# Output projections tile by tile, with logits held token by partition, in a two-layer attention and expert step on one core

## The chip, the cores and the metric

The kernel runs on one core of a Trainium2 chip. The metric is the device time of one execution in microseconds. Before the change the median of three runs is 1421.58 us (1417.67 to 1422.39).

## The reference

The step computes two layers for 512 prompt tokens and 64 sample tokens (8 sequences of 8), each of width 1024, in float32. Layer 0 mixes with forgetting attention (prompt, and samples against a paged cache), layer 1 with an mLSTM. After each mixer comes the part that the change touches:

```python
xp = xp + mixed_p @ w_out            # and the same for xs; 1024 x 1024
h  = rmsnorm(x, norm_ffn[layer])     # x * rsqrt(mean(x*x) + eps) * g
g_logits = h @ w_group + b_group     # 4 groups
e_logits = h @ w_router + b_router   # 4 x 8 experts
# best group, its two best experts, softmax weights of the two
# y = sum over the two experts of silu(h @ w_gate) * (h @ w_up) @ w_down
```

After the second layer a last rmsnorm gives the outputs. Keys, values, forget logs and states are outputs too; the change doesn't touch them.

## The kernel before

The program is a row of phases. In each, the five engines have an instruction list of their own, tied by semaphores, and all meet at its end. `out_and_experts` (L1020) is the phase after each mixer, so it runs twice. Tokens lie in five tiles: four of 128 prompt tokens (0 to 3) and one of 64 samples (tile 4, called L in the code). `turned` holds the mixer's result with features on partitions, in KC = 8 chunks; `x` and `rows` hold tokens on partitions. PSUM has eight banks of 512 floats; `ps2` views them as four pairs of 1024.

**Products.** `multiply_out` (L1225) runs over the eight chunks outside and the four prompt tiles inside, so all four tiles fill four bank pairs together and all are complete only in the last chunk. The samples follow in the pair of tile 0 once that was read: their two column halves lie in the two partition halves of the array. In layer 1 the weight chunks arrive from memory just ahead (L1128) and lie in the third expert slot; in layer 0 they were loaded in the phase before (`w0_in`).

**Norm.** For each tile: VectorE adds the product to `x` (`add_tile` L1469, `add_samples` L1474); ScalarE squares and sums (`square` L1396, which writes `rows` as scrap); VectorE makes the mean (`mean` L1456); GpSimd raises it to -0.5 (L1200); ScalarE scales `x` into `rows` (`scale` L1402); SyncE's queue stores `rows` to memory (`keep_row_tile` L1121), from where the experts' tokens are gathered later. TensorE flips the tile in eight transposes (`flip` L1244), and VectorE multiplies by the gain, back into `turned` (`keep_gained` L1461).

**Logits.** `logits` (L1258) multiplies with the router weights as the stationary operand (64 columns, of which 36 are used and 28 are cleared) and the tokens as the moving one. Even chunks go to the upper partition half and odd ones to the lower, so the result is logits by token, in two half sums. When all five tiles are in, VectorE adds the bias and copies them to SBUF (L1509), and TensorE adds the halves and turns them to tokens on partitions, with five products by a folding matrix (L1272). TensorE's order is written out by hand in `pe_` (L1330): products, flip 0, flip 1, then logits and flips alternately.

**Routes.** `routes` (L1482) on VectorE picks groups and experts, in small dependent steps from L1491 on, with TensorE counting ranks (L1276, L1278), building the lists (L1284) and the overflow lists (L1291). `idle_products` (L184) are products nobody reads, put between. Then GpSimd gathers the tokens of the first two pairs of experts (L1185), which waits for the lists (`index_ready`) and for all stored rows (`kept`).

**Experts.** Sixteen pairs of experts, of 6 MB of weights each, go through three slots. Pairs 0 and 1 are loaded at the phase's start. Pair 2's gate and up weights (L1140) wait for all products, since layer 1's output weights lie there, and its down weights (L1145) for all flips and for `kept`, since they overwrite `rows`. The gate and up weights of pair 3 wait for half of pair 0's products (`gu_half`, L1310), and so on, slot by slot.

Of the kernel before, what the change touches and what calls it, by code (L numbers as in the profile page):

```python
# [16 lines left out]
ALU = mybir.AluOpType  # L17
# [3 lines left out]
P = 128  # L21
# [95 lines left out]
def trunk(nc, i, o):  # L117

    with ExitStack() as ctx:
# [900 lines left out]
        def out_and_experts(layer, w_dram, w_early=None):  # L1020
# [5 lines left out]
            SLOTS = 3  # L1026
            gu = [sb(tag + f"gu{s}", [P, 2, 2, KC, HID], where=mx) for s in range(SLOTS)]
# [9 lines left out]
            lb = sb(tag + "lb", [P, 1], where=mx)  # L1037
# [14 lines left out]
                  for k, n in enumerate(("en", "ea", "both8"))}  # L1052
# [16 lines left out]
            cleared_, wr_in, lg_done, lT_kept, lg_turned = (sem(tag + "cleared"), sem(tag + "wr_in"), sem(tag + "lg_done"),  # L1069
                                                            sem(tag + "lT_kept"), sem(tag + "lg_turned"))  # L1070
# [50 lines left out]
            def keep_row_tile(sp, n):  # L1121

                sp.wait_ge(scaled, n + 1)
                sp.dma_start(h_dram[layer][n * P:n * P + ROWS[n], :], rows[0:ROWS[n], n, :]).then_inc(kept, 16)

            def sp_(sp):
                for c in range(KC if layer else 0):
                    sp.dma_start(w[:, c, :], w_dram[c * P:(c + 1) * P, :]).then_inc(w_in[c], 16)  # L1128
                sp.wait_ge(cleared_, 2)
                sp.dma_start(wr[:, :, 0:GROUPS], i["moe_w_group"][layer].rearrange("(p c) n -> p c n", c=KC)).then_inc(wr_in, 16)  # L1130
                sp.dma_start(wr[:, :, GROUPS:LG], i["moe_w_router"][layer].rearrange("(p c) n -> p c n", c=KC)).then_inc(wr_in, 16)
                sp.dma_start(lb[0:GROUPS, :], i["moe_b_group"][layer:layer + 1, :].rearrange("a n -> n a"), allow_slow_non_contiguous=True).then_inc(wr_in, 16)
                sp.dma_start(lb[GROUPS:LG, :], i["moe_b_router"][layer:layer + 1, :].rearrange("a n -> n a"), allow_slow_non_contiguous=True).then_inc(wr_in, 16)
# [91 lines left out]
            def multiply_out(pe):  # L1225

                if layer:
                    idle_products(pe, 4, 0)
                for c in range(KC):
                    pe.wait_ge(w_in[c], 16)  # L1230
                    for n in range(L):
                        for half in range(2):
                            mm = pe.matmul(ps[:, 2 * n + half, :], turned[:, c, n * P:(n + 1) * P],  # L1233
                                           w[:, c, half * 512:half * 512 + 512], start=(c == 0), stop=(c == KC - 1))
                        if c == KC - 1:
                            mm.then_inc(multiplied, 1)
                pe.wait_ge(added, 1)
                for c in range(KC):
                    for half in range(2):
                        mm = pe.matmul(ps[half * SAMP:(half + 1) * SAMP, half, :], turned[:, c, PROMPT:TOK],  # L1240
                                       w[:, c, half * 512:half * 512 + 512], start=(c == 0), stop=(c == KC - 1))
                mm.then_inc(multiplied, 1)

            def flip(pe, n):  # L1244

                r = ROWS[n]
                pe.wait_ge(scaled, n + 1)
                if n < 2:
                    pe.wait_ge(added, n + 2)
                elif n < L:  # L1250
                    pe.wait_ge(gained, n - 1)
                else:
                    pe.wait_ge(added, L + 2)
                for c in range(KC):
                    mm = pe.transpose(ps2[:, (1, 2, 1, 2, 0)[n], c * P:c * P + r], rows[0:r, n, c:D:KC], ident[0:r, 0:r])
                mm.then_inc(flipped, 1)

            def logits(pe, n):  # L1258

                r = ROWS[n]  # L1260
                pe.wait_ge(gained, n + 1)
                for c in range(KC):
                    half = c % 2
# [1350 lines left out]
```

## Time and profile before

| | |
|---|---|
| median of 3 runs | 1421.58 us |
| lowest, highest | 1417.67, 1422.39 us |
| profiled execution, its own time | 1428.57 us |
| span of its trace | 1426.7 us |
| TensorE products busy | 1237.4 us (87%) |
| TensorE weight loads busy | 654.8 us (46%) |
| VectorE, ScalarE, GpSimd busy | 26%, 17%, 15% |
| memory traffic | 322.18 MB read, 31.31 MB written |

A busy TensorE is one with a product in flight, idle products among them; its share says nothing of which stage sets the end. That is read from the chain of waits and from the timeline of the stage.

### The profile page before, as it was taken

How to read it: one execution, taken by the hardware profiler on the slowest of the kernel's cores; microseconds unless marked ns; L12 is line 12 of the kernel's file. 1: busy time of each engine (PE TensorE's matmuls, PEld its weight loads, DVE VectorE, ACT ScalarE, POOL GpSimd, SP SyncE). 2: the span in 40 equal slices, each digit the busy share in tenths (PEclk: the TensorE clock that was granted, in tenths of full speed). 3: DMA queues.
4: the chain of work that ended last, by engine and by line, in shares of the span. 5: the costliest groups of instructions: out<-in, count | busy, mean ns of one | idle time of the engine just before them, and what ended most of it. 6: DMA issues, size and time to landing. Idle time of an engine off the chain costs nothing.

```text
span 1426.7 us, 16246 instructions
## 1 busy us (share of the span) xinstructions
PE 1237.4 (87%) x6285; PEld 654.8 (46%) x6285; DVE 370.4 (26%) x793; ACT 246.7 (17%) x572; POOL 214.4 (15%) x268
## 2 busy tenths in 40 slices
PE   8999999879699899778868999998879989977790
PEld 5764575557444533233324764444744543333330
DVE  4231003545311621111114400112710541111115
ACT  2000004653200201000003201014410300100001
POOL 2300002322100111111001000212920011111102
PEclk9999999999999999988988999999989999998995
DMA  8320504859975689999957130303148579999965
GB/s 282 102 62 7 179 13 137 266 183 362 344 282 224 250 302 420 419 419 420 410 221 270 60 105 18 121 12 82 39 146 352 190 253 417 419 420 419 419 277 207
DMA packets 103676, 339.96 MB, mean 238 GB/s; under 512 B 21454, under 2 KB 40082, under 8 KB 79786
## 3 DMA queue, kind: packets, MB, share of 16 engines
q1 hardware_dynamic: 88456, 302.84, 55.8%
q0 software_dynamic: 14848, 35.94, 7.0%
q8 instruction: 53, 0.87, 0.3%
q14 instruction: 29, 0.24, 0.1%
q10 hardware_dynamic: 290, 0.07, 0.0%
HBM read 322.18 MB, written 31.31 MB: 248 GB/s over the span
## 4 chain that ended last, share of the span: by engine, by line
PE 54%; SPq 16%; DMA 12%; DVE 7%; issue 4%; POOL 3%; ACT 2%; POOLq 2%; DVEq 0%; ACTq 0%
SPq L1096 10%; PE ps L1819 8%; PE ps L1233 8%; PE ps L1308 7%; PE ps L458 4%; DMA moe_gu<-in_moe_w_up 4%; SPq L1118 4%; PE ps L436 4%; PE ps L1770 4%; DMA fox_arena<-negs_rows 3%; PE ps L1326 3%; PE ps L351 2%; DMA moe_wd<-in_moe_w_down 1%; PE ps L748 1%; PE ps L1830 1%
## 5 line engine op out<-in xcount | busy, mean ns | idle before, releaser
L1308 PE MATMUL ps<-moe_gu,rows 128*64 128x512 f32 x1024 | 243.6, 630 | 57.1 <-DMA moe_gu<-in_moe_w_up 53.8
L1308 PEld LDWEIGHTS ps<-moe_gu,rows 128*64 128x64 f32 x1024 | 80.5, 145 | 199.8 <-issue 191.1
L1819 PE MATMUL ps<-mwblk,turned 128*128 128x512 f32 x256 | 111.5, 593 | 2.2 <-DVE vaug L2022 1.5
L1595 DVE TENSOR_TENSOR turned<-turned,ps 128x256 f32<-128x256 f32 x32 | 13.5, 421 | 304.7 <-ACT turned L1411 304.7
L1192 POOL DMA_INDIRECT expert_rows<-turned,moe_row x32 | 32.1, 1004 | 392.3 <-ACT turned L1421 358.8
L1326 PE MATMUL ps<-moe_wd,moe_rowsel 128*64 128x512 f32 x352 | 80.4, 598 | 2.3 <-DMA moe_wd<-in_moe_w_down 1.3
L1819 PEld LDWEIGHTS ps<-mwblk,turned 128*128 128x128 f32 x256 | 48.0, 190 | 61.1 <-issue 57.4
L1411 ACT ACTIVATE turned<-ps 128x256 f32<-128x256 f32 x32 | 12.3, 384 | 302.4 <-PE ps L1308 302.4
L458 PE MATMUL ps<-turned,fox_arena 128*128 128x288 f32 x256 | 62.3, 406 | 0.0
L436 PE MATMUL ps<-fox_arena,turned 128*128 128x512 f32 x128 | 59.0, 619 | 2.9 <-issue 2.9
L1233 PE MATMUL ps<-fox_arena,turned 128*128 128x512 f32 x128 | 55.2, 593 | 0.7 <-DVEq L2564 0.7
L351 PE MATMUL ps<-turned,fox_arena 128*128 128x288 f32 x224 | 55.2, 406 | 0.0
L1233 PE MATMUL ps<-moe_gu,turned 128*128 128x512 f32 x128 | 55.2, 593 | 0.0
L458 PEld LDWEIGHTS ps<-turned,fox_arena 128*128 128x128 f32 x256 | 48.6, 190 | 14.1 <-issue 0.8
L1770 PE MATMUL ps<-turned,mwblk 128*128 128x288 f32 x224 | 54.5, 406 | 0.0
L237 POOL TENSOR_TENSOR fox_arena<-fox_arena,cst 128x256 f32<-128x256 f32 x32 | 23.0, 728 | 201.2 <-DMA fox_arena<-negc_rows 201.0
L186 PE MATMUL ps<-cst 128*128 128x512 f32 x68 | 40.0, 731 | 9.5 <-POOLq L2564 8.3
L1770 PEld LDWEIGHTS ps<-turned,mwblk 128*128 128x128 f32 x224 | 42.6, 190 | 11.8
L351 PEld LDWEIGHTS ps<-turned,fox_arena 128*128 128x128 f32 x224 | 42.2, 190 | 11.4
L1600 DVE COPY turned<-ps 128x512 f32<-128x512 f32 x32 | 22.1, 691 | 88.0 <-PE ps L1326 88.0
L1185 POOL DMA_INDIRECT turned<-h_rows,moe_row x32 | 33.2, 1038 | 76.6 <-DVE moe_row L1554 44.1
L928 DVE CUSTOM_DVE_ANT_0 fox_arena<-ps,fox_arena 128x128 f32<-128x128 f32 (+3 forms) x64 | 28.2, 479 | 62.9 <-PE ps L725 62.9
(357 smaller groups left out, 1567.5 us busy)
## 6 DMA issues: line engine op xcount, KB each, us to landing
moe_gu<-in_moe_w_gate SPq DMA_DIRECT2D x56, 1024.0 KB, 22.3
moe_gu<-in_moe_w_up SPq DMA_DIRECT2D x56, 1024.0 KB, 23.9
moe_wd<-in_moe_w_down SPq DMA_DIRECT2D x44, 1024.0 KB, 25.0
rows<-in_moe_w_down SPq DMA_DIRECT2D x20, 1024.0 KB, 22.9
fox_arena<-in_cache_v POOLq DMA_DIRECT2D x32, 512.0 KB, 13.1
fox_arena<-in_fox_w_in SPq DMA_DIRECT2D x6, 2048.0 KB, 10.3
mwblk<-in_mlstm_w_in SPq DMA_DIRECT2D x6, 2048.0 KB, 8.6
fox_arena<-in_cache_k SPq DMA_DIRECT2D x20, 512.0 KB, 9.7
```

What stands on the lines that cost most here:

```text
L186: pe.matmul(ps[:, bank, :], ident, const("ones")[:, 0:512], start=True, stop=True)
L351: mm = pe.matmul(ps[:, 2 * (g % 3) + half, 0:HT], wblk[:, g // 4, c, (g % 4) * P:(g % 4 + 1) * P], turned[:, c, half * HT:(half + 1) * HT] ...
L436: mm = pe.matmul(ps[:, m % 4, :], turned[:, c, n * P:(n + 1) * P], wblk[:, (2 + blk) % 3, c, :], start=(c == 0), stop=(c == KC - 1))
L458: mm = pe.matmul(ps[:, 2 * ((g + 2) % 4) + half, 0:HT], wblk[:, (4 + g // 4) % 3, c, (g % 4) * P:(g % 4 + 1) * P], turned[:, c, half * HT: ...
L1096: sp.dma_start(gu[p % SLOTS][:, half, k], i[name][layer, 2 * p + half].rearrange("(p c) n -> p c n", c=KC)).then_inc(gu_in[p % SLOTS], 16)
L1118: sp.dma_start(wd[p % SLOTS][:, half], i["moe_w_down"][layer, 2 * p + half].rearrange("(p c) n -> p c n", c=2)).then_inc(down_in[p % SLOTS ...
L1185: pool.indirect_dma_start(xg[:, s, :], None, h_dram[layer], bass.IndirectOffsetOnAxis(ap=rows_of(0, p), axis=0), bounds_check=TOK - 1, oob ...
L1233: mm = pe.matmul(ps[:, 2 * n + half, :], turned[:, c, n * P:(n + 1) * P], w[:, c, half * 512:half * 512 + 512], start=(c == 0), stop=(c == ...
L1308: mm = pe.matmul(ps[h, 2 + p % 2, :].rearrange("s (k f) -> s k f", k=2), xT[:, c, h], gu[s][:, half, :, c, :], start=(c == 0), stop=(c == ...
L1326: mm = pe.matmul(ps[h, 5 + n, :], aT[p % 2][:, m, h], wd[s][:, half, m, n * 512:(n + 1) * 512], start=(m == 0), stop=(m == 1))
L1770: mm = pe.matmul(ps[:, bank + half, 0:HT], wblk[:, k % 3, c, g * P:(g + 1) * P], turned[:, c, half * HT:(half + 1) * HT], start=(c == 0), ...
L1819: mm = pe.matmul(ps[:, m % 4, :], turned[:, c, n * P:(n + 1) * P], wblk[:, k % 3, c, :], start=(c == 0), stop=(c == KC - 1))
```

## The change

The five tiles are taken in the order 0, 1, 2, L, 3. The products of a tile run over all eight chunks before the next tile's begin, and TensorE's flips and logits of earlier tiles stand between them; the products of tile 3 are cut in two halves, with flip L and logits 2 between. Three bank pairs serve products and flips in turn. Logits have the tokens as the stationary operand (128 columns) and the router weights as the moving one (36 columns), and the bias comes in by a product of one row of ones with the bias row, so the result stands with tokens on partitions in bank 6; the copy to SBUF and the fold are gone. Clearing `wr` and `lb`, and SyncE's wait for it, are gone. Four idle products stand ahead of flip 3. In the diff `AT[n]` is a tile's place in the order, counted from 1. `ps2` pairs and `rows` are as before.

```diff
+            ORDER = (0, 1, 2, L, 3)
+            AT = {n: k + 1 for k, n in enumerate(ORDER)}
+            MUL_PAIR, TURN_PAIR = {0: 0, 1: 2, 2: 1, L: 0, 3: 2}, {0: 0, 1: 2, 2: 1, L: 0, 3: 1}
-            lb = sb(tag + "lb", [P, 1], where=mx)
+            lb = sb(tag + "lb", [1, LG], where=mx)
...
             def sp_(sp):
-                sp.wait_ge(cleared_, 2)
...
-                for n in range(L - 1):
+                for n in ORDER[0:NT - 1]:
                     keep_row_tile(sp, n)
                 sp.wait_ge(multiplied, NT)
                 load_gate_up(sp, 2)
-                keep_row_tile(sp, L - 1)
-                keep_row_tile(sp, L)
+                keep_row_tile(sp, ORDER[NT - 1])
...
             def pool_(pool):
-                pool.memset(wr[:], 0.0).then_inc(cleared_, 1)
-                pool.memset(lb[:], 0.0).then_inc(cleared_, 1)
-                for n in range(NT):
-                    pool.wait_ge(meaned, n + 1)
+                for n in ORDER:
+                    pool.wait_ge(meaned, AT[n])
...
+            def multiply_out(pe, n, chunks):
+                b = 2 * MUL_PAIR[n]
+                if n == L:
+                    pe.wait_ge(gained, AT[0])
+                elif n == 3:
+                    pe.wait_ge(gained, AT[1])
+                for c in chunks:
+                    pe.wait_ge(w_in[c], 16)
+                    for half in range(2):
+                        cols = slice(half * 512, half * 512 + 512)
+                        to = ps[:, b + half, :] if n < L else ps[half * SAMP:(half + 1) * SAMP, b + half, :]
+                        mm = pe.matmul(to, turned[:, c, n * P:n * P + ROWS[n]], w[:, c, cols], start=(c == 0), stop=(c == KC - 1))
+                if c == KC - 1:
+                    mm.then_inc(multiplied, 1)
+
+            def flip(pe, n):
+                r = ROWS[n]
+                pe.wait_ge(scaled, AT[n])
+                if n == 3:
+                    pe.wait_ge(gained, AT[2])
                 for c in range(KC):
+                    mm = pe.transpose(ps2[:, TURN_PAIR[n], c * P:c * P + r], rows[0:r, n, c:D:KC], ident[0:r, 0:r])
+                mm.then_inc(flipped, 1)
+
+            def logits(pe, n):
+                r = ROWS[n]
+                pe.wait_ge(gained, AT[n])
+                if r < P:
+                    pe.matmul(ps[r:P, 6, n * LG:(n + 1) * LG], const("ones", 1)[:, 0:P - r], lb[:], start=True, stop=True)
+                pe.matmul(ps[0:r, 6, n * LG:(n + 1) * LG], const("ones", 1)[:, 0:r], lb[:], start=True, stop=False)
                 for c in range(KC):
-                    half = c % 2
-                    mm = pe.matmul(psf[half * SLOT:(half + 1) * SLOT, 6 * 512 + n * P:6 * 512 + n * P + r], wr[:, c, :],
-                                   turned[:, c, n * P:n * P + r], start=(c < 2), stop=(c >= KC - 2))
+                    mm = pe.matmul(ps[0:r, 6, n * LG:(n + 1) * LG], turned[:, c, n * P:n * P + r], wr[:, c, 0:LG],
+                                   start=False, stop=(c == KC - 1))
                 mm.then_inc(lg_done, 1)
 
             def route(pe):
-                pe.wait_ge(lT_kept, 2)
-                for n in range(NT):
-                    mm = pe.matmul(ps[:, 0, n * LG:(n + 1) * LG], lT[:, n * P:(n + 1) * P], const("fold"), start=True, stop=True)
-                mm.then_inc(lg_turned, 1)
                 idle_products(pe, 5, 4)
...
             def pe_(pe):
-                multiply_out(pe)
+                if layer:
+                    idle_products(pe, 4, 7)
+                multiply_out(pe, 0, range(KC))
+                multiply_out(pe, 1, range(KC))
                 flip(pe, 0)
+                multiply_out(pe, 2, range(KC))
                 flip(pe, 1)
                 pe.wait_ge(wr_in, 64)
-                pe.wait_ge(added, L)
                 logits(pe, 0)
+                multiply_out(pe, L, range(KC))
                 flip(pe, 2)
                 logits(pe, 1)
+                multiply_out(pe, 3, range(KC // 2))
+                flip(pe, L)
+                logits(pe, 2)
+                multiply_out(pe, 3, range(KC // 2, KC))
+                logits(pe, L)
+                idle_products(pe, 4, 7)
                 flip(pe, 3)
-                logits(pe, 2)
-                flip(pe, 4)
                 logits(pe, 3)
-                logits(pe, 4)
                 route(pe)
...
             def act_(act):
+                for n in ORDER:
                     square(act, n)
+                    scale(act, n)
...
             def routes(dve):
                 dve.wait_ge(lg_done, NT)
-                dve.tensor_scalar(lT[:, 0:TOK], psf[:, 6 * 512:6 * 512 + TOK], lb[:, 0:1], None, ALU.add).then_inc(lT_kept, 1)
-                dve.wait_ge(lg_turned, 1)
-                lg = ps[:, 0, 0:NT * LG].rearrange("p (n e) -> p n e", e=LG)
+                lg = ps[:, 6, 0:NT * LG].rearrange("p (n e) -> p n e", e=LG)
...
             def dve_(dve):
+                add_tile(dve, 0)
+                mean(dve, 0)
+                add_tile(dve, 1)
+                keep_gained(dve, 0)
+                mean(dve, 1)
+                add_tile(dve, 2)
+                keep_gained(dve, 1)
+                mean(dve, 2)
+                add_tile(dve, L)
+                keep_gained(dve, 2)
+                mean(dve, L)
+                keep_gained(dve, L)
+                add_tile(dve, 3)
+                mean(dve, 3)
+                keep_gained(dve, 3)
                 routes(dve)
```

## Rows read from the trace of the kernel before

**Rows 1.** The page, the chain that ended last, shares of the span by line.
```profile
SPq L1096 10%; PE ps L1819 8%; PE ps L1233 8%; PE ps L1308 7%; PE ps L458 4%; DMA moe_gu<-in_moe_w_up 4%; SPq L1118 4%; PE ps L436 4%; PE ps L1770 4%; DMA fox_arena<-negs_rows 3%; PE ps L1326 3%; PE ps L351 2%; DMA moe_wd<-in_moe_w_down 1%; PE ps L748 1%; PE ps L1830 1%
```
**Rows 2.** The chain in order of time (start us, us, what), layer 0's phase.
```profile
408.42 55.17 PE ps L1233 x128
463.59 7.04 PE ps L1240 x32
...
569.60 2.89 SPq L1096
```
**Rows 3.** Timeline: start us, us, engine, line, tiles, records [idle before <-releaser]; both layers.
```profile
408.42 7.96 PE L1233 MATMUL ps<-fox_arena,turned 128*128 128x512 f32 x18 [0.70 <-DVEq L2564]
...
483.55 0.18 DVE L1491 TENSOR_REDUCE moe_gmax<-ps 128x5 f32<-128x20 f32 x1 [1.40 <-PE ps L1272]
...
1059.98 2.41 PE L1233 MATMUL ps<-moe_gu,turned 128*128 128x512 f32 x5
...
1135.15 0.18 DVE L1491 TENSOR_REDUCE moe_gmax<-ps 128x5 f32<-128x20 f32 x1 [1.40 <-PE ps L1272]
```
**Rows 4.** Timeline of layer 0, flips, logits and fold after the products.
```profile
470.54 2.05 PE L1255 MATMUL ps<-cst,rows 128*128 128x128 f32 x16
...
474.48 1.16 PE L1255 MATMUL ps<-cst,rows 128*128 128x128 f32 x8
475.57 1.09 PE L1264 MATMUL ps<-turned,moe_wr 128*64 128x128 f32 x16
...
481.34 0.82 DVE L1509 TENSOR_SCALAR moe_lT<-ps,moe_lb 128x576 f32<-128x576 f32 x1 [0.81 <-PE ps L1264]
...
482.21 1.30 PE L1272 MATMUL ps<-cst,moe_lT 128*128 128x36 f32 x10 [0.92 <-DVE moe_lT L1509]
...
483.35 4.54 PE L186 MATMUL ps<-cst 128*128 128x512 f32 x10
```
**Rows 5.** Timeline of layer 0, the norm's chain: one full tile's add, then the samples' steps.
```profile
460.19 1.22 DVE L1472 TENSOR_TENSOR x<-x,ps 128x1024 f32<-128x1024 f32 x1 [0.42 <-PE ps L1233]
...
472.09 1.06 ACT L1400 ACTIVATE rows<-x 64x1024 f32<-64x1024 f32 x1 [3.25 <-DVE x L1479]
...
473.50 0.55 POOL L1200 TENSOR_TENSOR rstd<-ms,cst 128x1 f32<-128x1 f32 x1 [5.94 <-DVE ms L1459]
...
474.08 1.15 ACT L1406 ACTIVATE rows<-x,rstd 64x1024 f32<-64x1024 f32 x1 [0.85 <-POOL rstd L1200]
...
475.68 1.23 DVE L1465 TENSOR_TENSOR turned<-ps,gains 128x1024 f32<-128x1024 f32 x1 [1.12 <-PE ps L1255]
```
**Rows 6.** Timeline of layer 0, SyncE's queue and GpSimd's gather.
```profile
470.64 0.33 SPq L1096 DMA_DIRECT2D moe_gu<-in_moe_w_gate  x1
...
472.79 2.97 SPq L1124 DMA_DIRECT2D h_rows<-rows  x2
...
487.88 0.81 SPq L1118 DMA_DIRECT2D rows<-in_moe_w_down  x2
...
496.10 1.14 POOL L1185 DMA_INDIRECT turned<-h_rows,moe_row  x1 [22.05 <-DVE moe_row L1554]
```
**Rows 7.** Output weights: timeline of their issues, then layer 1's median us to landing.
```profile
397.70 4.11 SPq L659 DMA_DIRECT2D fox_arena<-in_fox_w_out  x6
...
1054.71 5.55 SPq L1128 DMA_DIRECT2D moe_gu<-in_mlstm_w_out  x8
...
moe_gu<-in_mlstm_w_out SPq DMA_DIRECT2D x8, 512.0 KB, 7.9
```
**Rows 8.** Timeline, idle products and transposes where the granted clock is half.
```profile
494.79 3.56 PE L186 MATMUL ps<-cst 128*128 128x512 f32 x4
...
1051.55 1.97 PE L2273 MATMUL ps<-cst,mstaged 128*128 128x128 f32 x8 [6.28 <-DVE mstaged L2459]
```
**Rows 9.** One-us windows, layer 0: busy of PE, PEld, DVE, ACT, POOL; clock, DMA, GB/s.
```profile
478.00:479.00 1.00, 1.00 (x19) 0.83 (x13) 1.00 (x1) 0.00 (x0) 0.00 (x0) 1.00 1.09 451
...
491.00:492.00 1.00, 0.00 (x0) 0.00 (x0) 0.93 (x3) 0.00 (x0) 0.00 (x0) 0.59 0.98 410
```

More of the change, by code:

```diff
@@ L1121, in keep_row_tile @@
             def keep_row_tile(sp, n):
-                sp.wait_ge(scaled, n + 1)
+                sp.wait_ge(scaled, AT[n])
                 sp.dma_start(h_dram[layer][n * P:n * P + ROWS[n], :], rows[0:ROWS[n], n, :]).then_inc(kept, 16)
@@ L1423, in act_ @@
             def act_(act):
-                for n in range(L):
+                for n in ORDER:
                     square(act, n)
-                    if n:
-                        scale(act, n - 1)
-                scale(act, L - 1)
-                square(act, L)
-                scale(act, L)
+                    scale(act, n)
                 act.wait_ge(to_exp, 1)
@@ L1463, in keep_gained @@
                 r = ROWS[n]
-                dve.wait_ge(flipped, n + 1)
+                dve.wait_ge(flipped, AT[n])
                 dve.tensor_tensor(turned[:, :, n * P:n * P + r],
-                                  ps2[:, (1, 2, 1, 2, 0)[n], :].rearrange("p (c t) -> p c t", t=P)[:, :, 0:r],
+                                  ps2[:, TURN_PAIR[n], :].rearrange("p (c t) -> p c t", t=P)[:, :, 0:r],
                                   gain.unsqueeze(2).broadcast_to([P, KC, r]), ALU.mult).then_inc(gained, 1)
             def add_tile(dve, n):
-                dve.wait_ge(multiplied, n + 1)
-                dve.tensor_tensor(x[:, n, :], x[:, n, :], ps2[:, n, :], ALU.add).then_inc(added, 1)
-            def add_samples(dve):
-                dve.wait_ge(multiplied, NT)
-                for half in range(2):
-                    cols = slice(half * 512, half * 512 + 512)
-                    dve.tensor_tensor(x[0:SAMP, L, cols], x[0:SAMP, L, cols], ps[half * SAMP:(half + 1) * SAMP, half, :], ALU.add
-                                      ).then_inc(added, 1)
+                dve.wait_ge(multiplied, AT[n])
+                b = MUL_PAIR[n]
+                if n < L:
+                    ins = dve.tensor_tensor(x[:, n, :], x[:, n, :], ps2[:, b, :], ALU.add)
+                else:
+                    for half in range(2):
+                        cols = slice(half * 512, half * 512 + 512)
+                        ins = dve.tensor_tensor(x[0:SAMP, L, cols], x[0:SAMP, L, cols], ps[half * SAMP:(half + 1) * SAMP, 2 * b + half, :], ALU.add)
+                ins.then_inc(added, 1)
             def routes(dve):
@@ L1606, in dve_ @@
                     dve.wait_ge(x_again, 16 * (NT - 1))
-                for n in range(L):
-                    add_tile(dve, n)
-                    if n:
-                        mean(dve, n - 1)
-                mean(dve, L - 1)
-                add_samples(dve)
-                keep_gained(dve, 0)
+                add_tile(dve, 0)
+                mean(dve, 0)
+                add_tile(dve, 1)
+                keep_gained(dve, 0)
+                mean(dve, 1)
[4 more added lines that the diff above has]
+                keep_gained(dve, 2)
                 mean(dve, L)
-                for n in range(1, NT):
-                    keep_gained(dve, n)
+                keep_gained(dve, L)
+                add_tile(dve, 3)
+                mean(dve, 3)
+                keep_gained(dve, 3)
                 routes(dve)
```

38 lines of the change are left out of this document (6 added, 32 removed).

## The prediction

> **What bounds the kernel now.** I read the page first. In its chain that ended last, the largest line is the loading of expert weights, and the output products (L1233) hold 8% of the span [rows 1]. The chain in order of time then shows how the phase is tied together: products of the four prompt tiles, products of the samples, a chain of small steps, and from about 570 us on SyncE's issues of weights [rows 2]. From there memory sets the pace, but a slot is only free, and the stream only starts, once pair 0 of the experts has been multiplied. So whatever moves the start of pair 0 moves the whole stream behind it, one to one, and nothing later gives it back. The question is therefore one distance, read in the timeline: from the first output product to the first step of the routes on VectorE. It is 483.55 - 408.42 = 75.13 us in layer 0 and 1135.15 - 1059.98 = 75.17 us in layer 1 [rows 3]. The two layers do the same, so I work one out and double it.
>
> What fills the 75.13 us is TensorE. Its products end at 470.54, which is 62.12 us after the start. From there to 483.55 are 13.01 us, and they hold the flips and logits of all five tiles, back to back but for short waits, then the copy and the fold [rows 4]. The norm of tiles 0 to 3 is already hidden: adds, squares and scales run on the other engines while TensorE multiplies tile 3 and the samples. What the change puts "under" the products are flips and logits, and these are TensorE's own work. They can't run beside products on the same engine; they only change places with them. That is the core of my forecast.
>
> **The change, part by part.**
>
> Products: the same 62.12 us, in another order. Four prompt tiles take 55.17 us, 13.79 each, and the samples the rest [rows 2].
>
> Flips: eight transposes took from 474.48 to 475.57, so 1.09 us [rows 4]. Flips 0, 1, 2 and L now stand ahead of the last product: 4 x 1.09 = 4.36 us.
>
> Logits: their form is new. Before, a tile took 1.09 us (16 records of 64 stationary columns, 475.57 on) [rows 4]. Now it takes eight products with 128 stationary and 36 moving columns, and one more for the bias. The nearest row is the fold: 128 stationary and 36 moving columns, five products in 10 records, from 482.21 to the next engine row at 483.35 [rows 4]. That is 1.14 / 10 = 0.114 us a record, and 9 products make 18 records: 2.05 us a tile. The ends are 1.09 us (no dearer than before) and 18 x 1.09 / 8 = 2.45 us (as dear as a transpose record). I take 2.05, since shape and type are the same. Logits 0, 1 and 2 ahead of the last product: 6.15 us. The last product then ends 62.12 + 4.36 + 6.15 = 72.63 us after the start.
>
> Waits in that stretch: flip 0 needs the norm of tile 0, some 4.6 us after its products by the chain below, and has tile 1's 13.79 us for it. The same holds for flips 1, 2 and L, with 6.9 us at the least. Products into a reused bank pair wait for gains that VectorE ended several us earlier. All at nothing. Behind a wait that failed here, all of TensorE would queue, so this cover matters.
>
> The tail: tile 3 is now alone at the end, and its whole norm lies open. Handover to VectorE about 0.15; add 1.22; handover 0.1; from the start of the square to that of the power 473.50 - 472.09 = 1.41; to the scale 0.58; scale 1.15 [rows 5]. That is 4.61 us to scaled rows. Beside it run logits L (estimated 1.2, with half the columns) and four idle products (4 x 0.91 = 3.6 by ten records in 4.54) [rows 4]: 4.8 us, so they end with the chain and cost 0.2 at the most; I count nothing. Then handover 0.1, flip 3 until VectorE starts 475.68 - 474.48 = 1.20, the gain 1.23 [rows 4, 5], handover 0.14, and logits 3 with their drain 2.25. Tail: 9.53 us. The routes begin 72.63 + 9.53 = 82.16 us after the start, against 75.13: **7.03 us later in each layer.**
>
> Removed: the copy (L1509) and the fold, 483.55 - 481.34 = 2.2 us [rows 3, 4], which the sum has by leaving them out. The routes themselves keep their length; the five idle products start in the same relation to them. Clearing `wr` and `lb` was beside products and brings nothing.
>
> Queues: SyncE has stored the other four tiles by then, and issues pair 2's loads at the last product, then tile 3's rows. Before, loads issued at 470.64 and rows behind them until 475.76 let `kept` through at 487.88, 17.2 us later [rows 6]. Now the same bytes but the samples' follow, so `kept` comes some 17 us after 72.63, at 89.8 after the start. The gather's start was 496.10 - 408.42 = 87.7 [rows 6], and is 94.7 after. So 4.9 us of slack are left, where there were 8. Pair 2's down weights, held by the same wait, are sent 7 us before the gather now and 8 before; they may brush it. I put 0.2 us on each layer, between 0 and 1.5.
>
> First products: tile 0 now takes a weight chunk each 13.79 / 8 = 1.72 us, not each 6.9. In layer 0 the last chunks were issued by 401.81, and the last is needed at 420.5. In layer 1 the last is issued by 1060.3; chunks take 7.9 us to land, so 1068.2, and it is needed at 1072.0 [rows 3, 7]. Nothing at the one end; 1.5 us, once, at the other, if chunks 1 to 3 land together. I take nothing.
>
> **Sum.** 2 x (7.03 + 0.2) = 14.5 us. The profiled execution's own time is 1428.6 us (span 1426.7), which gives 1443.1. It lies 7.0 us above the median of 1421.58; the same steps on the median give **1436.0 us**, 1.0% slower.
>
> **A rule weighed.** While flips and logits ran without a break, the granted clock stayed at its upper level, as in the window at 478 us; it fell at 491 us, behind a stretch in which TensorE had little to do [rows 9]. The Trainium skill, TensorE: Matmul & The Clock Gate, in its part on PE-mode transpose, says that transposes don't count as busy in the way products do, so the clock would not rise for them. The first of these windows disagrees, as far as flips mixed with logits go.
>
> **The rivals.**
>
> *Cheap logits.* If 36 moving columns are what counts and a tile takes 1.09 us, four tiles save 4 x 0.96 = 3.8 us a layer, 7.7 in all: 1428.3 us. For it: fewer moving columns than before. Against it: the fold's records, of the same shape.
>
> *All hidden, so faster.* Weight loads are drawn beside products, and if the inserted flips and logits ran under the 512-column products at no cost, the routes would begin after 62.12 + 9.53 = 71.65 us, 3.5 earlier than now: 1421.6 - 7.0 = 1414.6 us. It decides if the inserted work costs under 3.5 us of its 10.5. Against it: flips and logits stood end to end with each other, 1.09 us each, never overlapped [rows 4]. This is the case on the other side.
>
> *The clock falls in the tail.* Tile 3's tail is sparse, as the stretch before 491 us was. At the lower level eight transposes took 1.97 us instead of 1.16 [rows 4, 8], the logits could take 2.05 more, and an idle record 0.89 instead of 0.45 [rows 4, 8], so five idle products could outlast the routes' first steps by some 3.7. All three together are 6.5 us a layer; I price half, 3.3: 1442.6 us. Against it: the four idle products stand just ahead. By the skill's rule above this case is likelier, since flip 3 would not hold the clock; that sentence moves no number.
>
> *`kept` takes over.* If the rows of tile 3, queued behind 4 MB of loads, take over 22 us instead of 17.2, GpSimd's gather waits for them, and everything behind it. At 24.5 us it is 2.4 a layer: 1440.8 us. Against it: the order and sizes in the queue are as before.
>
> *The change does less than it says.* If TensorE's reorder left the end of products where it is, and the tail alone grew or shrank to match the 13.0 us, the time would stay at 1421.6. Nothing in the rows gives that.
>
> **How the numbers follow.** Forecast 0.74 (own range 1432 to 1440, from the logits' upper end, 4 x 0.4 x 2 = 3.2, and the small terms), cheap logits 0.09, clock 0.08, `kept` 0.04, all hidden 0.03, no effect 0.02. The range runs from just under the cheap logits, 1428, to just over `kept`, 1442. About 0.3% is what a measurement of this kernel can tell from no change, 4.3 us. Faster 0.03, same 0.03, slower 0.94.
>
> **What would show it.** Right: the first step of the routes 82 us after the first output product in both layers; a full tile's logits near 2.05 us; TensorE without a wait from start to the last product at 72.6; square, power and scale of tile 3 with nothing of worth beside them; the weights' stream unchanged but 7 and 14 us later. Wrong: a distance of 78 (logits cheap) or under 75 (hidden), a clock at half level between the last product and the routes, or GpSimd's gather released by stored rows.

## The result and the profile after the change

The changed kernel takes 1443.33 us (median of 4 runs, 1431.42 to 1445.92) against 1421.46 us before. The ratio is 1.0137, with a 95% interval from 1.0092 to 1.0182: **slower by 1.4%**, some 19.5 us by the ratio. The profiled execution took 1445.92 us, its span is 1443.8 us.

The first thing to read is the same distance as before, from the first output product to the first step of the routes, and then on to pair 0 of the experts. The timeline of layer 0 on TensorE (start us, us, engine, line, tiles, records, idle before):

```profile
404.56 27.70 PE L1235 MATMUL ps<-fox_arena,turned 128*128 128x512 f32 x64 [0.71 <-DVEq L2557]
432.10 1.05 PE L1246 MATMUL ps<-cst,rows 128*128 128x128 f32 x8
...
446.72 1.05 PE L1246 MATMUL ps<-cst,rows 128*128 128x128 f32 x8
447.70 0.41 PE L1255 MATMUL ps<-moe_lb,cst 1*128 1x36 f32 x2
448.04 1.98 PE L1257 MATMUL ps<-moe_wr,turned 128*128 128x36 f32 x16
449.94 7.09 PE L1235 MATMUL ps<-fox_arena,turned 128*64 128x512 f32 x32
...
460.19 7.11 PE L1235 MATMUL ps<-fox_arena,turned 128*128 128x512 f32 x16
467.24 1.09 PE L1246 MATMUL ps<-cst,rows 64*128 64x64 f32 x8
...
470.40 8.81 PE L1235 MATMUL ps<-fox_arena,turned 128*128 128x512 f32 x16
479.14 0.24 PE L1254 MATMUL ps<-moe_lb,cst 1*64 1x36 f32 x1
...
480.43 3.70 PE L186 MATMUL ps<-cst 128*128 128x512 f32 x8
483.97 1.04 PE L1246 MATMUL ps<-cst,rows 128*128 128x128 f32 x8
486.33 0.41 PE L1255 MATMUL ps<-moe_lb,cst 1*128 1x36 f32 x2 [1.32 <-DVE turned L1457]
486.67 2.46 PE L1257 MATMUL ps<-moe_wr,turned 128*128 128x36 f32 x16
488.94 7.45 PE L186 MATMUL ps<-cst 128*128 128x512 f32 x10
...
509.60 5.80 PE L1297 MATMUL ps<-moe_gu,rows 128*64 128x512 f32 x26 [0.74 <-DVE rows L1578]
```

From the first product to the end of logits L at 480.43 us no row has idle time before it, so TensorE is the bound of that stretch, as forecast. Behind it stand the four idle products, beside the norm of tile 3. Flips and logits stand between the products, each with its own time. The two halves of tile 3's products are the same work, but the first runs from 460.19 to 467.24 (7.05 us) and the second from 470.40 to 479.14 (8.74 us). The last product ends 74.58 us after the start, not 72.63.

VectorE, SyncE's queue and GpSimd around the tail, the same timeline:

```profile
479.25 1.22 DVE L1466 TENSOR_TENSOR x<-x,ps 128x1024 f32<-128x1024 f32 x1 [10.19 <-PE ps L1235]
479.25 0.34 SPq L1098 DMA_DIRECT2D moe_gu<-in_moe_w_gate  x1
...
482.50 1.15 ACT L1402 ACTIVATE rows<-x,rstd 128x1024 f32<-128x1024 f32 x1 [0.84 <-POOL rstd L1198]
...
489.17 0.18 DVE L1482 TENSOR_REDUCE moe_gmax<-ps 128x5 f32<-128x20 f32 x1 [2.89 <-PE ps L1257]
...
495.20 0.80 SPq L1120 DMA_DIRECT2D rows<-in_moe_w_down  x2
...
502.56 1.13 POOL L1185 DMA_INDIRECT turned<-h_rows,moe_row  x1 [20.10 <-DVE moe_row L1543]
```

The routes begin 489.17 - 404.56 = 84.61 us after the start, against 75.13 [rows 3]. Layer 1 shows the same, on TensorE and VectorE:

```profile
1066.65 27.63 PE L1235 MATMUL ps<-moe_gu,turned 128*128 128x512 f32 x64
...
1132.42 8.81 PE L1235 MATMUL ps<-moe_gu,turned 128*128 128x512 f32 x16
...
1151.04 0.18 DVE L1482 TENSOR_REDUCE moe_gmax<-ps 128x5 f32<-128x20 f32 x1 [2.74 <-PE ps L1257]
...
1172.54 7.82 PE L1297 MATMUL ps<-moe_gu,rows 128*64 128x512 f32 x32
```

There it is 84.39 us. Where pair 0 of the experts began before, in the chain that ended last (start us, us, what):

```profile
503.13 7.09 PE ps L1308 x32
...
1154.73 7.09 PE ps L1308 x32
```

From the start to pair 0 it was 94.71 and 94.75 us before; now it is 105.04 and 105.89. That is 10.33 + 11.14 = 21.5 us more, and the median rose by 21.9. What follows pair 0 kept its length: from layer 0's pair 0 to layer 1's first product it was 556.85 us and is 557.05, and from layer 1's pair 0 to the end of the span 272.0 and 271.3. So a later pair 0 did move the whole stream, one to one. The spans differ by only 17.1, because the attention part ahead of layer 0 happened to end 3.9 us earlier in this execution.

Why tile 3's second half is slower stands in windows of one us (window, its length, then busy of PE, PEld, DVE, ACT, POOL; granted clock; DMA share; GB/s):

```profile
470.00:471.00 1.00, 1.00 (x8) 0.76 (x8) 0.00 (x0) 0.00 (x0) 0.00 (x0) 0.96 0.00 0
471.00:472.00 1.00, 1.00 (x3) 0.48 (x2) 0.00 (x0) 0.00 (x0) 0.00 (x0) 0.50 0.00 0
...
475.00:476.00 1.00, 1.00 (x3) 0.38 (x2) 0.00 (x0) 0.00 (x0) 0.00 (x0) 1.00 0.00 0
...
487.00:488.00 1.00, 1.00 (x11) 1.00 (x10) 0.00 (x0) 0.00 (x0) 0.00 (x0) 0.99 0.97 410
488.00:489.00 1.00, 1.00 (x7) 1.00 (x6) 0.00 (x0) 0.00 (x0) 0.00 (x0) 0.50 0.97 393
```

TensorE is busy in every one of the windows shown, and yet the granted clock falls to half, 1.2 GHz, at about 471 us, right behind flip L and logits 2, and again at 488 us, within logits 3. Ahead of the second fall TensorE had waited 1.32 us for tile 3's gain. It is this second fall that stretches the five idle products to 7.45 us from 4.54 [rows 4].

### The profile page after: what moved, and what is told of

It is laid out like the page before. It is cut to its first block, busy times and chain, and to the rows that moved or that the text cites. A ratio compares the mean times of both kernels' runs of the same rounds, so it can differ in the third digit from the quotient of the medians.

```text
span 1443.8 us, 16270 instructions
## 1 busy us (share of the span) xinstructions
PE 1271.4 (88%) x6305; PEld 679.8 (47%) x6305; DVE 369.6 (26%) x789; ACT 248.2 (17%) x572; POOL 212.5 (15%) x264
## 4 chain that ended last, share of the span: by engine, by line
PE 56%; SPq 15%; DMA 12%; DVE 5%; issue 4%; POOL 3%; ACT 2%; POOLq 2%; DVEq 0%; ACTq 0%
PE ps L1235 9%; SPq L1098 9%; PE ps L1812 8%; PE ps L1297 7%; SPq L1120 5%; PE ps L458 4%; DMA moe_gu<-in_moe_w_up 4%; PE ps L436 4%; PE ps L1763 4%; DMA fox_arena<-negs_rows 3%; DMA moe_wd<-in_moe_w_down 3%; PE ps L1315 2%; PE ps L186 2%; PE ps L351 2%; PE ps L748 1%
## 5 line engine op out<-in xcount | busy, mean ns | idle before, releaser
L1297 PE MATMUL ps<-moe_gu,rows 128*64 128x512 f32 x1024 | 250.0, 644 | 50.2 <-DMA moe_gu<-in_moe_w_up 47.6
L1235 PE MATMUL ps<-fox_arena,turned 128*128 128x512 f32 (+1 forms) x160 | 64.6, 606 | 0.7 <-DVEq L2557 0.7
L1235 PE MATMUL ps<-moe_gu,turned 128*128 128x512 f32 (+1 forms) x160 | 64.5, 605 | 0.0
L186 PE MATMUL ps<-cst 128*128 128x512 f32 x84 | 52.3, 770 | 9.6 <-POOLq L2557 8.3
L436 PE MATMUL ps<-fox_arena,turned 128*128 128x512 f32 x128 | 57.4, 605 | 2.9 <-issue 2.9
L1315 PEld LDWEIGHTS ps<-moe_wd,moe_rowsel 128*64 128x64 f32 x352 | 23.7, 136 | 44.1 <-issue 41.6
```

The source lines that it names most:

```text
L186: pe.matmul(ps[:, bank, :], ident, const("ones")[:, 0:512], start=True, stop=True)
L436: mm = pe.matmul(ps[:, m % 4, :], turned[:, c, n * P:(n + 1) * P], wblk[:, (2 + blk) % 3, c, :], start=(c == 0), stop=(c == KC - 1))
L1235: mm = pe.matmul(to, turned[:, c, n * P:n * P + ROWS[n]], w[:, c, cols], start=(c == 0), stop=(c == KC - 1))
L1297: mm = pe.matmul(ps[h, 2 + p % 2, :].rearrange("s (k f) -> s k f", k=2), xT[:, c, h], gu[s][:, half, :, c, :], start=(c == 0), stop=(c == ...
L1315: mm = pe.matmul(ps[h, 5 + n, :], aT[p % 2][:, m, h], wd[s][:, half, m, n * 512:(n + 1) * 512], start=(m == 0), stop=(m == 1))
```

## The experiments

All were timed in five rounds beside the kernel before. **Theory 1** is the prediction's: TensorE's own work and the open norm chain of tile 3 set the distance. **Theory 2** came from the profile after: flips with logits of only 36 moving columns are followed by a fall of the clock. e5 to e7 were planned on the results of e1 to e4, and e8 and e9 on those of e5 to e7.

**e1, the form of the logits alone, in the old order.**

```diff
+                pe.matmul(ps[0:r, 6, n * LG:(n + 1) * LG], const("ones", 1)[:, 0:r], lb[:], start=True, stop=False)
                 for c in range(KC):
-                    half = c % 2
-                    mm = pe.matmul(psf[half * SLOT:(half + 1) * SLOT, 6 * 512 + n * P:6 * 512 + n * P + r], wr[:, c, :],
-                                   turned[:, c, n * P:n * P + r], start=(c < 2), stop=(c >= KC - 2))
+                    mm = pe.matmul(ps[0:r, 6, n * LG:(n + 1) * LG], turned[:, c, n * P:n * P + r], wr[:, c, 0:LG],
+                                   start=False, stop=(c == KC - 1))
...
-                for n in range(NT):
-                    mm = pe.matmul(ps[:, 0, n * LG:(n + 1) * LG], lT[:, n * P:(n + 1) * P], const("fold"), start=True, stop=True)
...
-                dve.tensor_scalar(lT[:, 0:TOK], psf[:, 6 * 512:6 * 512 + TOK], lb[:, 0:1], None, ALU.add).then_inc(lT_kept, 1)
```

> The old order of work with the new form of the logits alone (tokens stationary, 36 moving columns, bias by a product, no copy, no fold). Theory 1, TensorE's own work sets the distance: a full tile's logits cost 2.24 us as in the changed kernel instead of 1.09, less 2.2 us of copy and fold, so the first step of the routes comes about 16.4 us after the last product instead of 13.0: 3.4 us more a layer, about 1428 us against 1421.5. Theory 2, the 36-column logits are too thin to hold the granted clock: the 16 us of flips and logits, or the idle products behind them, run partly at half level, and the time is 1432 to 1438 us, with windows at 0.5 in that stretch where the kernel before has 1.00. Rival, the new form is free and only the order cost: 1421 us.

Measured: 1443.85 us, ratio 1.0162 (1.0133 to 1.0190). The form alone costs as much as the whole change. Windows of five us of e1:

```profile
465.00:470.00 5.00, 4.14 (x30) 3.93 (x29) 2.65 (x4) 2.30 (x3) 0.54 (x1) 0.83 0.92 380
470.00:475.00 5.00, 5.00 (x24) 4.60 (x23) 1.22 (x1) 0.00 (x0) 0.00 (x0) 0.50 0.99 377
475.00:480.00 5.00, 5.00 (x23) 4.60 (x24) 1.23 (x1) 0.00 (x0) 0.00 (x0) 0.50 0.64 225
480.00:485.00 5.00, 5.00 (x27) 4.74 (x27) 0.69 (x1) 0.00 (x0) 0.00 (x0) 0.50 0.36 119
```

and two rows of its timeline:

```profile
470.98 0.64 PE L1260 MATMUL ps<-moe_lb,cst 1*128 1x36 f32 x2
...
474.98 1.95 PE L1251 MATMUL ps<-cst,rows 128*128 128x128 f32 x8
```

The clock falls within the first tile's logits and stays down through all the flips and logits that follow. There a tile's logits take 4.0 us (470.98 to 474.98), not 2.24, and a flip 1.88. Theory 2's numbers were still too low: it expected 1432 to 1438.

**e2, the order alone.** The changed kernel with the old logits, clearing, copy and fold, taken back as in the diff of the change. Its four idle products go to bank 0, since bank 7 holds L's logits.

```diff
                 logits(pe, L)
-                idle_products(pe, 4, 7)
+                idle_products(pe, 4, 0)
```

> The new order of products, flips and logits, with the old form of the logits, copy and fold. Theory 1: the end of products comes 62.1 + 4 flips + 3 logits of 1.09 = 69.4 us after the start, the open chain of tile 3 and copy and fold bring the first step of the routes to about 80.5 us, 5.4 a layer more than before: about 1432 us, and the granted clock stays at 1.00 through all products. Theory 2 as above, the thin logits are what lowers the clock: same 1432, and the changed kernel's half-level stretch in tile 3's products is gone. Rival, the order itself (flips parting the products) lowers the clock: half level in tile 3's products here too, and about 1436 to 1440 us.

Measured: 1428.97 us, ratio 1.0058 (1.0037 to 1.0079). The distance to the routes is 79.80 us in layer 0 and 80.67 in layer 1, where 80.5 were expected. Timeline of e2 on TensorE, tile 3's two halves in layer 0, and the fold and the idle products in layer 1:

```profile
455.55 7.13 PE L1239 MATMUL ps<-fox_arena,turned 128*128 128x512 f32 x16
...
464.67 7.13 PE L1239 MATMUL ps<-fox_arena,turned 128*128 128x512 f32 x16
471.73 0.69 PE L1259 MATMUL ps<-turned,moe_wr 128*64 128x64 f32 x16
...
1137.46 2.35 PE L1267 MATMUL ps<-cst,moe_lT 128*128 128x36 f32 x10 [0.92 <-DVE moe_lT L1506]
1139.61 6.73 PE L186 MATMUL ps<-cst 128*128 128x512 f32 x10
```

Both halves take the same time, so with the old logits the order doesn't lower the clock in tile 3's products. Behind them it does. In the open tail TensorE waits three times (0.24, 1.32 and 0.92 us in layer 0), and the clock falls to half in both layers, at the end of layer 0's fold and just ahead of layer 1's. Layer 1's fold takes 2.35 us, against 1.30 before [rows 4], and the five idle products 6.17 and 6.73 us, against 4.54. That is why layer 1's distance is the longer one; at 79.80 us the order costs 4.7 us a layer, a little less than theory 1's 5.4.

**e3, held back.** The flips and logits that are ready go behind the last product and cover tile 3's norm.

```diff
                 multiply_out(pe, L, range(KC))
+                multiply_out(pe, 3, range(KC))
                 flip(pe, 2)
                 logits(pe, 1)
-                multiply_out(pe, 3, range(KC // 2))
                 flip(pe, L)
                 logits(pe, 2)
-                multiply_out(pe, 3, range(KC // 2, KC))
-                logits(pe, L)
-                idle_products(pe, 4, 7)
                 flip(pe, 3)
+                logits(pe, L)
                 logits(pe, 3)
...
                 add_tile(dve, L)
-                keep_gained(dve, 2)
                 mean(dve, L)
-                keep_gained(dve, L)
                 add_tile(dve, 3)
+                keep_gained(dve, 2)
                 mean(dve, 3)
+                keep_gained(dve, L)
                 keep_gained(dve, 3)
```

> The changed kernel, but flip 2, logits 1, flip L and logits 2 stand behind the last product, where they cover the norm of tile 3, and the four idle products are gone; VectorE takes the gains of 2 and L behind the add of tile 3. Theory 1, an open norm chain is the price of the order: the last product ends about 66 us after the start and the first step of the routes comes at about 77.5 us instead of 84.5, with no wait of TensorE on the scaled rows of tile 3; about 1427 us. Theory 2: the now long stretch of flips and thin logits loses the clock and half the gain: 1430 to 1436 us. Rival, the chain is not what costs: no faster than the changed kernel, 1440 us or more.

Measured: 1435.47 us, ratio 1.0101 (1.0079 to 1.0123), distances 81.00 and 80.46. TensorE has no wait in the stretch, so the open chain is covered, but the clock fell at 477 us, within the flips and logits behind the last product, and took back about half, as theory 2 said. Timeline of e3, the last flip and logits:

```profile
477.42 1.95 PE L1246 MATMUL ps<-cst,rows 128*128 128x128 f32 x8
...
482.08 3.63 PE L1257 MATMUL ps<-moe_wr,turned 128*128 128x36 f32 x16
485.51 7.25 PE L186 MATMUL ps<-cst 128*128 128x512 f32 x10
```

**e4, flip L and logits 2 parted** by a quarter of tile 3's products.

```diff
                 flip(pe, L)
+                multiply_out(pe, 3, range(KC // 2, 3 * KC // 4))
                 logits(pe, 2)
-                multiply_out(pe, 3, range(KC // 2, KC))
+                multiply_out(pe, 3, range(3 * KC // 4, KC))
```

> The changed kernel, but the two pieces that stand together inside tile 3's products, flip L and logits 2, are parted by a quarter of those products. Same work. Theory 2, a thin stretch of 3.2 us ahead of the second half of tile 3 is what lowers the clock: it stays at 1.00 through tile 3, which ends 1.85 us earlier in each layer, about 3.7 us less than the changed kernel in the same clock condition elsewhere, so about 1439.5 us. Theory 1 alone expects the same time as the changed kernel, 1443 us. Rival, the fall only moves to another thin stretch: same time, half level elsewhere.

Measured: 1435.49 us, ratio 1.0115 (1.0092 to 1.0138). The two quarters take 3.63 and 3.61 us, start to start, in both layers, at a clock of 1.00 in layer 0's windows. The distances are 82.62 and 83.32 us. Timeline of e4 in layer 0, the start, the idle products and the first step of the routes:

```profile
399.92 27.71 PE L1235 MATMUL ps<-fox_arena,turned 128*128 128x512 f32 x64 [0.70 <-DVEq L2558]
...
482.33 4.54 PE L186 MATMUL ps<-cst 128*128 128x512 f32 x10
482.54 0.18 DVE L1483 TENSOR_REDUCE moe_gmax<-ps 128x5 f32<-128x20 f32 x1 [2.40 <-PE ps L1257]
```

The fall in tile 3's products is gone in both layers, as theory 2 said. The second fall is gone in layer 0, where the idle products take 4.54 us, and stays in layer 1, where they take 7.15. The time, 4 us below the expected 1439.5, agrees in its direction, but its interval overlaps with that of the changed kernel.

**e5, wide logits in the old order.** This is the decisive one: e1 with 100 moving columns (50 router columns, twice) instead of 36. The 64 columns beyond the 36 are not used.

```diff
+                twice = lb[:].unsqueeze(1).broadcast_to([1, 2, 50])
...
-                pe.matmul(ps[0:r, 6, n * LG:(n + 1) * LG], const("ones", 1)[:, 0:r], lb[:], start=True, stop=False)
+                pe.matmul(ps[0:r, 6, n * 100:(n + 1) * 100], const("ones", 1)[:, 0:r], twice, start=True, stop=False)
                 for c in range(KC):
-                    mm = pe.matmul(ps[0:r, 6, n * LG:(n + 1) * LG], turned[:, c, n * P:n * P + r], wr[:, c, 0:LG],
-                                   start=False, stop=(c == KC - 1))
+                    mm = pe.matmul(ps[0:r, 6, n * 100:(n + 1) * 100], turned[:, c, n * P:n * P + r],
+                                   wr[:, c, 0:50].unsqueeze(1).broadcast_to([P, 2, 50]), start=False, stop=(c == KC - 1))
```

> As e1 (old order, new form of the logits), but each logits product and its bias move 100 columns instead of 36 (50 router columns twice; the 64 columns beyond the 36 are not used). The stationary loads, 0.107 us a record in e1, stay; a record may take up to 0.136 us as a transpose does, so at a full clock the stretch would be up to 0.5 us a tile dearer than e1's 2.24 at full clock. Theory 2, the few moving columns of the logits lower the clock: flips and logits stand at 1.00 as in the kernel before, the first step of the routes comes about 79 to 80 us after the first product instead of e1's 86 to 87, and the time is 1429 to 1432 us against e1's 1443.9. Rival, what lowers it is the loads of 128 stationary columns at every record, or the length of the stretch: half level again and 1444 us or more.

Measured: 1429.29 us, ratio 1.0077 (1.0059 to 1.0095). Nearly three times the moving columns made the kernel 14.6 us faster. The same windows, of e5:

```profile
465.00:470.00 5.00, 4.14 (x36) 3.86 (x34) 2.95 (x4) 2.30 (x3) 0.54 (x1) 1.00 0.97 367
470.00:475.00 5.00, 5.00 (x41) 4.58 (x40) 2.45 (x2) 0.00 (x0) 0.00 (x0) 1.00 0.98 382
475.00:480.00 5.00, 5.00 (x44) 4.51 (x44) 0.69 (x1) 0.00 (x0) 0.00 (x0) 1.00 0.70 247
```

TensorE and its loads are as busy as in e1 (4.58 of 5 us in loads against 4.60), but 41 records fit where 24 did. Theory 2 holds, and the rivals (128 stationary columns at each record, the length of the stretch) fall, since both are the same in e5. The runs without a profile say the same: the mean clock over the span is 0.929 to 0.937 in all five runs of e1 and 0.944 to 0.954 in all six of e5. One thing besides the width differs. e5 clears `wr` and `lb` again and has SyncE's wait for it, as the kernel before, since 14 of the 50 columns hold no weights; no run tests this alone. The expectation's 0.107 us a record is no row of e1: a record there takes 0.113 us at full clock (1.81 / 16) and 0.215 at half (3.44 / 16), start to start.

**e6, the kernel before with two small edits**, the try at beating both.

```diff
-                pe.wait_ge(lT_kept, 2)
                 for n in range(NT):
+                    pe.wait_ge(lT_kept, 2 if n < L else 3)
...
                 mm.then_inc(rank_done, 1)
+                idle_products(pe, 2, 4)
...
+                dve.wait_ge(lg_done, L)
+                dve.tensor_scalar(lT[:, 0:PROMPT], psf[:, 6 * 512:7 * 512], lb[:, 0:1], None, ALU.add).then_inc(lT_kept, 1)
                 dve.wait_ge(lg_done, NT)
-                dve.tensor_scalar(lT[:, 0:TOK], psf[:, 6 * 512:6 * 512 + TOK], lb[:, 0:1], None, ALU.add).then_inc(lT_kept, 1)
+                dve.tensor_scalar(lT[:, PROMPT:TOK], psf[:, 7 * 512:7 * 512 + SAMP], lb[:, 0:1], None, ALU.add).then_inc(lT_kept, 1)
```

> The kernel before with two small edits: bias copy and fold of tiles 0 to 3 go under the logits of L, so that only L's 64 columns are left behind them, and two idle products fill TensorE's wait of 2.1 us between ranks and lists. Theory: the first step of the routes comes 0.8 us earlier; the clock no longer falls ahead of the lists, which take 1.36 instead of 2.35 us; 1.8 us a layer, 1416 us against 1419.9. Rival, the idle products outlast the wait, or the clock falls elsewhere in the routes: 1418 to 1421 us.

Measured: 1417.80 us, ratio 0.9987 (0.9971 to 1.0002): not told from no change. Timeline of e6 in layer 0:

```profile
485.89 1.36 PE L1285 MATMUL ps<-moe_tilesel,moe_rowsel 128*64 128x32 f32 x40 [0.18 <-DVE moe_rowsel L1550]
...
493.16 1.97 PE L1299 MATMUL ps<-cst,turned 128*128 128x128 f32 x8
```

The lists became cheap, 1.36 us, but the fall came later and took the first transposes of the experts (1.97 us, against 1.16 at the upper level [rows 4]). Start to pair 0 is 93.83 us in layer 1, 0.9 less than before, and 94.44 in layer 0, 0.3 less.

**e7, three idle products ahead of the ranks** in the changed kernel, not five.

```diff
-                idle_products(pe, 5, 4)
+                idle_products(pe, 3, 4)
```

> The changed kernel with three idle products instead of five ahead of the ranks. Theory, at half level the five outlast VectorE's first steps (TensorE came to the ranks 2.0 us after they were ready in layer 0, 0.5 in layer 1): the ranks start as soon as they are ready, about 2.5 us less in all, 1441 us against 1443.3. Rival, the freed time is lost again because the clock stays low through ranks and lists: 1443 us.

Measured: 1440.81 us, ratio 1.0136 (1.0114 to 1.0158). The median is 2.5 us lower, the ratio is that of the changed kernel: not resolved. In layer 0 the ranks do start on time:

```profile
490.48 5.09 PE L186 MATMUL ps<-cst 128*128 128x512 f32 x6
495.78 0.59 PE L1265 MATMUL ps<-moe_both,cst 128*128 128x192 f32 x2 [0.20 <-DVE moe_both L1512]
```

**e8, the changed kernel with the wide logits, and e9, e3 with them.** The edit is that of e5, with the clearing and SyncE's wait.

> The changed kernel with 100 moving columns in the logits products, as in e5. This takes the clock's fall out of the change and leaves its order and its work. Theory 1 with the prediction's own sum: products stand at 1.00 throughout, the last ends about 72.8 us after the first, the first step of the routes comes at 82.3 us, 7.2 us a layer over the kernel before, so 1434 us, about 9 less than the changed kernel. Rival, clock falls have other causes here (the open chain of tile 3): still half level at tile 3's products or at the idle products, 1440 us or more.

> e3 (flips and logits held back behind the last product, no idle products there) with 100 moving columns. Theories 1 and 2 together: nothing is open and the clock holds, so TensorE's own work is all that is left: first step of the routes at 78.2 us, 3.0 a layer over the kernel before: 1426 us, 9 less than e3. Rival, a wait on tile 3's gain or another engine is behind it: 1430 us or more.

e8: 1436.82 us, ratio 1.0124 (1.0098 to 1.0151), distances 83.30 and 83.31. e9: 1425.63 us, ratio 1.0046 (1.0028 to 1.0064), distances 78.23 and 78.15, where 78.2 were expected. Timeline of e8, tile 3's second half and the first step of the routes, layer 0:

```profile
467.03 7.05 PE L1238 MATMUL ps<-fox_arena,turned 128*128 128x512 f32 x16
474.01 0.29 PE L1258 MATMUL ps<-moe_lb,cst 1*64 1x100 f32 x1
...
484.21 0.18 DVE L1486 TENSOR_REDUCE moe_gmax<-ps 128x5 f32<-128x20 f32 x1 [2.51 <-PE ps L1261]
```

The changed kernel's half-level stretch is gone in e8, and so is its second fall: the five idle products take 4.48 us in both layers, though TensorE still waits 1.32 us for tile 3's gain. The expected distance of 82.3 left out the width of the logits, and the time is 3 us above the 1434 that it gave. Against the changed kernel the ratio's interval still overlaps, so that gain rests on the trace; between e1 and e5, and between e3 and e9, it stands in the times too. Layer 1's distances of all of them, in us:

| kernel | distance | median us |
|---|---|---|
| before | 75.17 | 1419.7 to 1421.5 |
| e9 held back, wide | 78.15 | 1425.6 |
| e5 old order, wide | 79.09 | 1429.3 |
| e3 held back | 80.46 | 1435.5 |
| e2 order alone | 80.67 | 1429.0 |
| e8 changed, wide | 83.31 | 1436.8 |
| e4 changed, parted | 83.32 | 1435.5 |
| changed | 84.39 | 1443.3 |
| e1 form alone | 85.94 | 1443.9 |

## Why the prediction was right, and where it was short

**The core was right.** Flips and logits under the products on the same engine hide nothing. Two kernels show the prediction's own case, with the clock level up to the routes. Layer 0 of e4 has the narrow logits: 82.62 us from start to routes, against a sum of 82.16 and 75.13 before, and its tail, 482.54 - 473.00 = 9.54 us, is that of the sum, 9.53. e8 takes 83.3 us in both layers. About 1.0 of that is the price of the width: a tile's logits take 0.11 us more in e8, four times, and those of L 0.55 more, behind which the idle products and flip 3 wait. Order and work thus cost 7.2 to 7.5 us a layer, where 7.03 were forecast. e2 and e9 part it as theory 1 does: the order alone takes the distance from 75.1 to 79.8 in layer 0, where the fold is not yet slow, and with the chain of tile 3 covered the work of e8 comes down from 83.3 to 78.2, 5.1 us.

**Products, flips.** The products take their 62 us, but for the 1.7 that the clock added. Flip 0, ahead of a product, takes 0.89 us (432.10 to 432.99), and those of 1, 2 and L, ahead of logits, 0.98, 1.09 and 1.02, where 1.09 was put for each: 3.98 us in all, not 4.36.

**Logits.** The term was mis-sized a little: 447.70 to 449.94 is 2.24 us, and logits 1 and 2 take 2.14 each, against 2.05. That is 6.52 us for the three, not 6.15. The fold row was the right one to go by: a record takes 1.80 / 16 to 1.90 / 16, 0.113 to 0.119 us, against 0.114 [rows 4]. The two bias records take 0.17 each, which is what the term had too low. By luck flips and logits together came to 10.50 us, where 10.51 was put. The rival of cheap logits falls.

**Tail.** To scaled rows: 482.50 + 1.15 - 479.14 = 4.51 us, against 4.61. The idle products end 0.3 us later than the rows, so they cost nearly nothing, as said. The tail is 10.03 us against 9.53; nearly all the excess is the second fall of the clock within logits 3, as e4's 9.54 without it shows.

**The step that was missing** is the one that has no line in the sum: that products, logits and routes keep the upper level of the clock. It stood only as a rival, with 0.08, its place put in the sparse tail of tile 3 and its price at 3.3 us a layer. Its price was about right: 1.7 us in tile 3's second half (8.74 against the first half's 7.05), 0.4 in logits 3, and the way from routes to pair 0 at 20.43 and 21.50 us, against 19.58 before. The place of the first and dearer fall ahead of the routes, and its reason, were wrong: it came in tile 3's products, where TensorE had been busy without a gap, and it followed the logits' 36 moving columns, which I had priced only by their loads. The second fall came where the rival put it, and with it the named sign of being wrong, a clock at half level between the last product and the routes (0.50 in the window at 488 us). What brings it about is not settled. e2 has such a fall with the old logits and more waits, e8 has none with wide logits and the same wait of 1.32 us, and e4, narrow, has it in one layer of two.

With the falls the median is 1443.3, just past the range's upper end of 1442.0; the ratio on the median before gives 1440.9. That the ratio's time is within the range owes to the width that the rivals gave it: the forecast's own range ended at 1440.

**The rule weighed.** The Trainium skill, TensorE: Matmul & The Clock Gate, in its part on PE-mode transpose, says that transposes don't count as busy as products do. Here the same flips stand at 1.00 where their neighbours are wide (e2, e5, e9: windows at 1.00 through all flips and logits) and at half level where they are narrow (e1). No run here has a long stretch of transposes alone, so the rule by itself stays open; between e1 and e5 the flips are the same, so they were not what made the difference.

**`kept`.** It came 495.20 - 479.25 = 16.0 us after the loads that stand ahead of it, at 90.6 us after the start (forecast 89.8), and the gather still waited for its lists, until 502.56. That rival falls. So do "all hidden" and "no effect". **First products:** no wait for a weight chunk in either layer, as put.

**Sum.** The two distances grew by 9.48 + 9.22 = 18.7 us. Order and work are about 2 x 7.2 of that, and the clock ahead of the routes the rest, 4.3 (2 x 2.1 by the two prices above). From routes to pair 0 come 0.85 and 1.92: 21.5 us in all. The forecast had 14.5 of it.

What stays open, besides the second fall: how often the clock falls in a run that was not profiled. The changed kernel's four runs have clocks of 0.940, 0.940, 0.943 and 0.949 over the span, and the last of these is the one of 1431.42 us. That fits an execution with less of the fall, but no trace shows it.

## What to carry to other kernels

Work of the bounding engine can't be hidden under other work of that engine. Before reordering, ask which engine does each moved step, and what last chain the new order leaves open: here the norm chain of one tile, 5.1 us a layer, which the old order had covered with the flips of the others.

Turning a product so that its result lies the right way can swap a wide moving operand for a narrow one. Price both the loads of the stationary side and what stands around it at the clock that is then granted; a few unused columns may be cheaper than none, as 14.6 us between e1 and e5 show. Here that only made the loss smaller: no kernel with the new form came below the one before, the best of them, e9, being 0.5% slower.

## What the runs showed of the hardware

The granted clock fell to 1.2 GHz while TensorE had no idle time at all: in the changed kernel no row behind the first product, 404.56 us, had idle time before it up to the fall at 471, and in e1 the windows from 470 to 485 us are fully busy and stand at 0.50. With 100 moving columns in place of 36 the same stretch stood at 1.00 (e5), at a cost per record of 0.117 us instead of 0.113 (1.87 / 16 and 1.81 / 16, both at full clock, start to start). At the lower level a record with 128 stationary and 36 moving columns took 0.215 us (e1, 3.44 / 16), 1.9 times as long, so the clock sets loads too.

It also fell with the old logits of 128 moving columns: in e2, behind waits of 0.24, 1.32 and 0.92 us ahead of flip, logits and fold, the clock stood at half from the fold on in both layers (6.17 and 6.73 us for the five idle products, against 4.54). That the waits did it is not shown.
